# Norm's weight row as one row spread by TensorE, first products reordered, fewer unread products

## The reference

```
h = RMSNorm(x) * g_pre_mix        # g_pre_mix: one row of 1024, the same for all positions
proj = h @ w_in                   # (1024 x 1024) @ (1024 x 2824)
```

## Time and profile before

| | |
|---|---|
| median of 3 runs | 1207.2 us (1206.07 to 1207.38) |
| profiled execution | 1209.47 us, span 1207.5 us |
| PE busy | 1173.1 us, 97% of the span, 6014 instructions |
| PEld busy | 992.9 us, 82% |
| DVE busy | 803.8 us, 67% |
| ACT busy | 540.5 us, 45% |
| POOL busy | 386.7 us, 32% |
| granted TensorE clock, mean | 0.993 of full speed |
| DMA | 181.89 MB, 151 GB/s on average |

### The profile page before, as it was taken

How to read it: one execution, slowest core, us unless ns; L and a number is a source line. 1 busy time by engine, 2 the same in 40 slices (tenths; PEclk the granted TensorE clock), 3 DMA queues, 4 the chain that set the end, 5 groups by cost and what they waited for, 6 DMA issues and landing times.

```text
span 1207.5 us, 17014 instructions
## 1 busy us (share of the span) xinstructions
PE 1173.1 (97%) x6014; PEld 992.9 (82%) x6014; DVE 803.8 (67%) x1144; ACT 540.5 (45%) x974; POOL 386.7 (32%) x349
## 2 busy tenths in 40 slices
PE   9999999998899999989899999999999999999997
PEld 8888888887788888877688888888888877888886
DVE  6432355467766677768977778778787777664557
ACT  6221153556355444436644544445444444553451
POOL 1221000211133332221356586556855551000001
PEclk9999999999899999999999999999999999999999
DMA  8321133546232323231144443644435466997513
GB/s 286 129 89 71 58 102 107 158 139 218 81 117 70 107 78 116 66 97 63 70 175 139 175 168 146 210 150 164 165 149 210 139 217 242 361 371 234 192 55 140
DMA packets 118296, 181.89 MB, mean 151 GB/s; under 512 B 20527, under 2 KB 78671, under 8 KB 113999
## 3 DMA queue, kind: packets, MB, share of 16 engines
q1 hardware_dynamic: 118223, 180.94, 44.5%
HBM read 123.21 MB, written 57.70 MB: 150 GB/s over the span
## 4 chain that ended last, share of the span: by engine, by line
PE 44%; DVE 3%; POOL 2%; issue 1%; DMA 1%; ACT 1%; SPq 0%; DVEq 0%; POOLq 0%; ACTq 0%
PE f_ps_up L3019 6%; PE f_ps_up L3020 5%; PE f_ps_up L3021 5%; PE sums L3019 5%; PE sums L3020 5%; PE sums L3021 5%; PE f_ps_up L3092 3%; PE f_ps_up L3094 3%; PE f_ps_up L3093 3%; PE sums L3094 2%; PE sums L3092 2%; PE sums L3093 2%; DMA stage<-in_w_down 1%; POOL conv L2979 1%; DVE f_rest_raw L2796 0%
## 5 line engine op out<-in xcount | busy, mean ns | idle before, releaser
L2975 POOL TENSOR_TENSOR f_w_raw<-stage 128x512 f32<-128x512 f32 x42 | 66.9, 1594 | 115.7 <-PE f_ps_up L3021 114.9
L2719 DVE TENSOR_TENSOR f_w<-f_w_raw,f_w 128x512 fp32r<-128x512 f32 (+1 forms) x54 | 68.2, 1283 | 33.6 <-POOL f_w_raw L2975 33.6
L2979 POOL TENSOR_TENSOR conv<-conv 128x512 f32<-128x512 f32 x44 | 70.8, 1609 | 28.1 <-DMA conv<-in_w_down 25.5
L2979 POOL TENSOR_TENSOR f_conv<-f_conv 128x512 f32<-128x512 f32 x44 | 66.4, 1508 | 33.9 <-DMA y_blocks<-f_conv 30.5
L233 PE MATMUL sums<-split,slab_w 128*128 128x512 f32 x192 | 75.9, 395 | 0.5 <-PEq L284 0.5
L235 PE MATMUL sums<-split,slab_w 128*128 128x512 f32 x192 | 74.9, 390 | 0.0
L234 PE MATMUL sums<-split,slab_w 128*128 128x512 f32 x192 | 74.7, 389 | 0.0
L3019 PE MATMUL f_ps_up<-split,f_w 128*128 128x512 f32 x176 | 69.6, 395 | 2.9 <-DVEq L2715 2.2
L254 DVE SCALAR_TENSOR_TENSOR conv<-sums,conv_taps,conv 128x1023 f32<-128x1023 f32 (+6 forms) x39 | 46.7, 1199 | 37.3 <-ACT conv L245 36.4
L2519 ACT CAST f_w<-f_w_raw 128x512 fp32r<-128x512 f32 (+1 forms) x54 | 42.7, 790 | 60.1 <-POOL f_w_raw L2975 60.1
L3020 PE MATMUL f_ps_up<-split,f_w 128*128 128x512 f32 x176 | 69.1, 392 | 0.0
(11 more groups left out here) (441 smaller groups left out, 3465.9 us busy)
## 6 DMA issues: line engine op xcount, KB each, us to landing
stage<-in_w_up SPq DMA_DIRECT2D x22, 1024.0 KB, 5.6
y_blocks<-f_conv SPq DMA_DIRECT2D x22, 1024.0 KB, 5.0
conv<-in_w_down SPq DMA_DIRECT2D x11, 1024.0 KB, 7.4
w_down_sums<-conv SPq DMA_DIRECT2D x11, 1024.0 KB, 10.5
stage<-y_blocks SPq DMA_DIRECT2D x40, 256.0 KB, 5.5
f_rest_raw<-y_blocks SPq DMA_DIRECT2D x37, 256.0 KB, 5.7
x_tile<-in_x SPq DMA_DIRECT2D x12, 512.0 KB, 4.3
stage<-in_w_in SPq DMA_DIRECT2D x6, 1024.0 KB, 6.4
```

The lines of the kernel that those rows point to most:

```text
L2719: dve.tensor_tensor(out, src, hi.bitcast(F32), ALU.subtract).then_inc(s_lo[name], 1)
L2975: pool.tensor_tensor(raw_sum(m), a, b, op).then_inc(s_add[m], 1)
L2979: pool.tensor_tensor(view(out), view(a), view(b), op).then_inc(signal, 1)
```

## The change

- SP loads `g_pre_mix` as one row into one partition of `row` (`gain_row`, behind the zeroed columns) instead of spreading it over 128.
- VectorE sets a row of 128 ones in partition 0 of the `gain` buffer (`one_row`) as its first instruction.
- TensorE runs 10 unread products, waits for the row, multiplies the ones (one contraction row) with the two halves of the row in plain F32, into the two banks of `ps_own`, so that every partition there has the row, and runs 4 more unread products. The 7 between `front(0, 0)` and `first_tiles` are gone. The unread products write to `kept.sums[:, 3]`.
- The norm of tile 0 takes the row from PSUM (`gain_ps`). ScalarE copies it to `gain` in SBUF, after the square of tile 1 and ahead of chunk 4's cast; the norms of the other tiles wait for that copy (`GAIN_KEPT`).
- VectorE makes the low part of tile 0 ahead of chunk 0's.
- TensorE begins `first_tiles` with chunk 0's two products with the tile's high part, as soon as its first half (`s_hi` 1) and the chunk's high part are there, and does the two with the tile's low part after them. Chunks 1 to 3 go as before.

```diff
--- before.py
+++ after.py
@@ -296,6 +296,7 @@
         h = sb("h", [P, D])
         row = sb("row", [P, ROW])
         gain = kept.conv[:, 1]
+        gain_row, one_row = row[0:1, 2 * P:2 * P + D], kept.conv[0:1, 1, 0:P]
         junk = kept.conv[:, 0, 0:HALF].bitcast(BF16)
         rest = kept.conv[:, 0, HALF:]
         rope = rest[:, 0:T * ROT].rearrange("p (t c r) -> p t c r", c=2, r=ROT // 2)
@@ -318,6 +319,8 @@
 
         ps_t = ctx.enter_context(nc.psum_tensor("ps_t", [P, 2, HALF], F32))
         ps_own = ctx.enter_context(nc.psum_tensor("ps_own", [P, 2, HALF], F32))
+        gain_ps = ps_own[:].rearrange("p b n -> p (b n)")
+        GAIN_IN, GAIN_SPREAD, GAIN_KEPT = 16, 18, 19
         row_sums = lambda n: kept.sums[:, n] if n < 4 else ps_own[:, n - 4]
         gate_sums = ps_t[:, 1, 0:2 * T * H]
         cum_turned = ps_t[:, 1, P:2 * P]
@@ -368,7 +371,7 @@
         @block.sync
         def _(sp):
             sp.dma_start(xin[0], x_tiles[0]).then_inc(s_x[0], 16)
-            sp.dma_start(gain, io["g_pre_mix"][0:1, :].broadcast_to([P, D])).then_inc(s_gain, 16)
+            sp.dma_start(gain_row, io["g_pre_mix"][0:1, :]).then_inc(s_gain, 16)
             sp.dma_start(ident, io["tables"][:, T_ID:T_ID + P]).then_inc(s_const, 16)
 
             def load_chunk(c):
@@ -520,6 +523,8 @@
                     keep_hi(0, 0)
                 if c == READY[0] - 1:
                     square(1, 1, 1)
+                    act.wait_ge(s_h, 1)
+                    act.copy(gain, gain_ps).then_inc(s_gain, 1)
                 if c == READY[1] - 1:
                     keep_hi(1, 1)
             tiles(act, tile)
@@ -556,6 +561,7 @@
 
         @block.vector
         def _(dve):
+            dve.memset(one_row, 1.0)
             dve.memset(row[:, 0:2 * P], 0.0).then_inc(s_mid, 1)
             for q in (s_z, s_last):
                 dve.sem_inc(q, 1)
@@ -570,10 +576,13 @@
                 dve.tensor_scalar(st[:, 1:2], st[:, 0:1], 1.0 / D, EPS, ALU.mult, ALU.add).then_inc(s_ms, 1)
                 dve.wait_ge(s_rstd, t + 1)
                 if isinstance(t, int) and t == 0:
-                    dve.wait_ge(s_gain, 16)
+                    dve.wait_ge(s_gain, GAIN_SPREAD)
+                    by = gain_ps
                 else:
+                    dve.wait_ge(s_gain, GAIN_KEPT)
                     dve.wait_ge(s_tr, 2 * t)
-                dve.scalar_tensor_tensor(h[:], xin[par], st[:, 2:3], gain, ALU.mult, ALU.mult).then_inc(s_h, 1)
+                    by = gain
+                dve.scalar_tensor_tensor(h[:], xin[par], st[:, 2:3], by, ALU.mult, ALU.mult).then_inc(s_h, 1)
 
             def keep_lo(t, par):
                 for b in range(2):
@@ -608,13 +617,12 @@
                 dve.tensor_tensor(x2, rot[:, 2], rot[:, 3], ALU.add).then_inc(s_rot, 1)
 
             norm(0, 0)
+            keep_lo(0, 0)
             for c in range(NCH):
                 g, k0, nk = CHUNKS[c]
                 dve.wait_ge(s_whi, c + 1)
                 dve.tensor_tensor(group_w(g, 1)[:, k0:k0 + nk], raw_chunk(c),
                                   group_w(g, 0)[:, k0:k0 + nk].bitcast(F32), ALU.subtract).then_inc(s_wlo, 1)
-                if c == 0:
-                    keep_lo(0, 0)
                 if c == READY[0] - 1:
                     norm(1, 1)
                 if c == READY[1] - 1:
@@ -674,10 +682,14 @@
         def _(pe):
             def unread(count):
                 for _ in range(count):
-                    pe.matmul(ps_own[:, 0, 0:P], row[:, 0:P], row[:, P:2 * P], start=True, stop=True)
+                    pe.matmul(kept.sums[:, 3, 0:P], row[:, 0:P], row[:, P:2 * P], start=True, stop=True)
 
             pe.wait_ge(s_mid, 1)
-            unread(18)
+            unread(10)
+            pe.wait_ge(s_gain, GAIN_IN)
+            for b in range(2):
+                pe.matmul(ps_own[:, b], one_row, gain_row[:, b * HALF:(b + 1) * HALF], start=True, stop=True).then_inc(s_gain, 1)
+            unread(4)
             pe.wait_ge(s_const, 16)
 
             def front(t, par):
@@ -702,8 +714,14 @@
                 return op
 
             def first_tiles():
+                pe.wait_ge(s_hi, 1)
+                pe.wait_ge(s_whi, 1)
+                for k in range(2):
+                    pe.matmul(kept.sums[:, 0], tile_hi[:, 0, k], group_w(0, 0)[:, k], start=(k == 0), stop=False)
                 pe.wait_ge(s_lo, 1)
-                for c in range(4):
+                for k in range(2):
+                    pe.matmul(kept.sums[:, 0], tile_lo[:, 0, k], group_w(0, 0)[:, k], start=False, stop=False)
+                for c in range(1, 4):
                     pe.wait_ge(s_whi, c + 1)
                     if c == 2:
                         pe.wait_ge(s_lo, 2)
@@ -752,7 +770,6 @@
                         front(t + 1, 1 - par)
 
             front(0, 0)
-            unread(7)
             first_tiles()
             with pe.Fori(1, T // 2 - 1) as i:
                 tile(i * 2, 0)
```

## The result

The changed kernel takes 1209.85 us (median of 9 runs, 1207.33 to 1212.64) against 1207.2 before (9 runs, 1206.07 to 1210.57): ratio 1.0021, interval 1.0012 to 1.003. Slower by 2.6 us, where 1207.8 was forecast; the time lies just above the range (1205.9 to 1209.6) and just on the slower side of the 0.2% bound. Its profiled execution is of 1210.86 us, span 1208.8.

A forecast was written before the change was run, and what follows sets the result against it. TensorE, busy 97% of the span, was taken as the bound. 1.23 us late at h, with 0.6 to 0.7 left at 21.5 us, gave +0.6 on 1207.2, so 1207.8 us; range 1205.9 to 1209.6.

The forecast's parts named there:

- Part 1: Start, transfer queue: 4 KB replace 512 KB, so chunk 0 lands at 6.4 to 7.1 us instead of 8.42.
- rival C: Start, transfers: the row lands as late as the old one, at 6.5 us; total 1208.4 us; chance 0.12.
- Part 2: TensorE's spreading of the row ahead of h: spread ends at 7.75 us, h is done 1.23 us later than before.
- Parts 2 to 4: Spread, first products' order and ScalarE's kept row: 1.23 us late at h, 0.6 to 0.7 us left at 21.5.
- rival B: Start, TensorE: clock stays at 1.2 GHz until about 13.3 us; 3.0 us slower in all, 1210.2 us; chance 0.08.
- real products at half clock in the first 15 us: Sign at the start, TensorE: the prediction would be wrong if its real products ran so; no size given.
- Its sentence on the seven unread products behind the transposes: TensorE behind the transposes: taking these products out costs nothing by itself; idle no more than 0.4 us at a time.
- The range of the rise: Start, TensorE's clock: rise taken at 6.4 us as one draw; spread ends between 7.35 and 8.98 us.
- Part 3: First products, chunks 0 to 3: the early start's gain is lost again to ScalarE's casts; size 0.
- Part 4: ScalarE's copy of the row before chunk 4's cast: 1.06 us; TensorE stands 0.4 us, group 1 ends 22.1 against 21.47.
- Whatever is late at 22 us is late at 100 us: Behind group 1: the shift at 22 us is still there at 100 us; sum +0.6 us.

The follow-up runs named there:

- e0_again: The changed kernel once more, unaltered: 1209.22 us, ratio 1.0012.
- e8: e7 with two one-row products of 512 columns, result unread, in place of eight of its 22 unread products: 1209.55 us.
- e7: The kernel before with the new order of the first products, 22 unread products ahead of the transposes and none behind: 1207.24 us.
- e10: The changed kernel with the row spread by full-width products (128 contraction rows, 127 of them zeros), its transfer behind the table: 1207.54 us.
- e5: The kernel before with 14 instead of 18 unread products and none behind the transposes: 1210.19 us, ratio 1.0025.
- e6: The changed kernel with 7 instead of 10 unread products ahead of the spread and the 7 behind the transposes back: 1210.53 us, ratio 1.003.
- e0_look: Another profile of the changed kernel, unaltered: profiled execution 1214.07 us.
- e2: The changed kernel with 7 instead of 4 unread products behind the spread and the 7 behind the transposes back: 1208.14 us, ratio 1.0009.
- e9: The changed kernel with VectorE's order undone, tile 0's low part behind chunk 0's: 1211.21 us, ratio 1.0028.
- e1: The kernel before with only the new order of VectorE's low parts and TensorE's first products: 1207.53 us, ratio 1.0004.
- e4: The changed kernel without ScalarE's copy; a spread transfer behind x tile 1 brings the row for tiles 1 to 7: 1209.29 us, ratio 1.0023.
- e13: e10 with ScalarE's copy moved behind chunk 0's cast and VectorE's order undone: 1207.92 us, ratio 1.0009.
- e11: e10 without ScalarE's copy (a second, spread transfer brings the row) and with VectorE's order undone: 1209.04 us, ratio 1.0009.
- e12: e11 with 7 instead of 10 unread products ahead of the spread and 7 instead of 4 behind it: 1209.49 us, ratio 1.0018.
- e14: e13 with 7, 7 and 4 unread products ahead of the spread, behind it and behind the transposes: 1206.94 us, ratio 1.0003.

## Why the prediction was wrong

- **Part 1, the transfers.** Half right: the row was there before the ten unread products ended, so rival C fell. But chunk 0 was cast from 7.73 (7.57 in e0_again), with its transfer as releaser, where 6.4 to 7.1 was worked out from 8.42: about half of the gain. It cost nothing here, because h came later still.
- **Part 2, the length of the spread and h.** Right in its result: start 1.33 (1.3), spread 5.66 (5.57), h 7.76 (7.85). A one-row product takes the time of its columns: four halves in 1.98 us at the upper level with the last one's pipeline. That h agrees so well is partly luck. The clock rose at 5.35 and not at 6.4, for which the prediction's own sum gives an end of 7.35 and not 7.75; a start 0.1 later and the 0.2 of the last one's pipeline, both left out, made up for most of it.
- **Parts 2 to 4, the clock: here it failed.** The whole sum stands on a clock that rises near 6.4 and stays at the upper level through the transposes and first products. The argument for it, held against rival B, was that TensorE is shown as full as before; it took TensorE's busy time for what holds the clock, and the thinner filling was put at nothing. The runs show that filling with one-row products doesn't hold it as full-width filling does: e8 against e7 (+1.75 us), e10 against the changed kernel (1207.54 against 1209.85 and 1209.22). In two of three profiles of the changed kernel there are 3.4 us at half clock through the transposes (0.9 us more for them; 0.3 and 0.9 us late at the slabs, where 0.6 was forecast). In the third the clock isn't up till 14.0, and the slabs are 3.2 us late. The prediction names it itself: real products at half clock in the first 15 us. Its sentence on the seven unread products behind the transposes fares better by itself: e7 has none there, but 22 ahead, and loses nothing. Taken out together with four of the 18 ahead they cost 2.9 us (e5), and for that the prediction had no term.
- **The range of the rise.** I weighed the rule of the Trainium skill that the rise differs from run to run ("TensorE: Matmul & The Clock Gate", "What's actually happening") and kept the spread's end within bounds for it. The traces agree (4.15, 5.35, and 14.0 for the same kernel), but the far one is beyond what I had bounded: h at 9.80. In e6 and e0_look the one-row products began before the rise, and it came 9.3 and 8.1 us after they had begun. That isn't so each time: in e2 and e9 they also began before it, at 5.90, and it came at 6.19 and 6.03.
- **Rival B** had the mechanism, its decision point (no upper level at the spread's end) and nearly its time (1210.2, 3.0 late; the slabs are 3.2 late in e0_look and 2.95 in e6, which ran 1210.5), and I gave it 0.08. What I held against it, that TensorE is as full as before, is the busy column again. Its milder form, a fall after a normal rise, wasn't among my cases.
- **The range.** By its own terms its upper end is 1207.2 + 1.9 + 0.65 = 1209.75 and not 1209.6, and it left rival B out. It took the scatter from three runs (1.3 us); nine runs of the same kernel scatter by 4.5.
- **Part 3, the order: 0.** Right in the total, too low by itself: e1 has chunk 4 0.6 us sooner and the slabs 0.25. So what is gained ahead of chunk 4 doesn't come through one for one, as the prediction has it.
- **Part 4, ScalarE's copy.** The size at the end of group 1 is right (22.25 for 22.1), the cause by half: VectorE's low part of chunk 3 came at 17.01, not 16.4, and binds as late as chunk 4's cast (17.5). e4 without the copy is held by the low part, e9 with VectorE's order undone by the cast; in e13, with both moved, neither binds.
- **Whatever is late at 22 us is late at 100 us.** Right: +0.9 at the slabs.

The mean over the changed kernel's 21 timed runs is 1209.6 us, that of e2, with late h and a filling that held the clock in its profile, 1208.45, and of e10 1207.62. With the spread at full width the slowdown is gone from the total, so the one-row products make nearly all of it. Three things stay open: in which executions and stages the loss falls (the profiles with an ordinary rise show 0.3 to 0.9 us of it at the slabs), why e5 with full-width products alone is as slow, and how e10's late h (slabs at 129.28) is made up for.

## What to carry over

Make filling products like the real ones, of 128 rows of contraction: with one-row products in the filling seven of eight profiles here lost the clock or got it late, whatever the busy time said. Before a wait on an engine's product is put ahead of the first real work, work it out at the lower clock too, and look at more than one profile, because the clock rose at 4.15, 5.35 and 14.0 us in three executions of one kernel. A copy or a transfer moved out of one queue was paid in the next one (e4, e11, e12) unless it went to a gap that a timeline shows (e13, e14).

## What the runs showed of the hardware

- One-row products in plain F32 of 512 columns are as long as their columns (two products: 1.98 us at 2.4 GHz in the changed kernel, 3.78 at 1.2 GHz in e0_look, with the last one's pipeline). Behind a filling with them the clock was at half for 3.4 us (from 7.6, 8.8 or 9.4 us; 8.8 in e4 and e8 too), or didn't rise until 13.9 to 14.0 us (e6, e0_look); e2, with three more full-width products behind the spread and seven behind the transposes, had neither.
- With 127 rows of zeros added (e10) and as many columns the clock stayed up, with 2.75 us busy of the 3.41 behind its rise; in e5 it stayed up with 1.85 of 3.41, while it fell behind 3.38 (changed kernel) and 3.41 (e8) with one-row products. Zeros as data did not cost it: the unread products of e7 are zeros as well.
